# Attention of a hybrid diffusion block: the next unit's scores are written between the second and the third group of turned probabilities

## What is computed

```python
# A, windowed: local keys within +-128 tokens, context keys, a sink
s_loc = einsum('bnqgrd,bnkgd->bngrqk', qb, kb); s_loc = where(mask, s_loc, NEG_INF)
s_ctx = einsum('bnqgrd,bkgd->bngrqk', qb, kc)
p = softmax(concatenate([s_loc, s_ctx, s_sink], -1), -1)
o = p[..., :nk] @ vb + p[..., nk:nk + L] @ vc
# B, neighbourhood: all 512 latent keys with bias and mask, and context keys
s_nb = einsum('brqhd,brwkhd->brhqwk', qg, kg) + bias; s_nb = where(col_ok, s_nb, NEG_INF)
p = softmax(concatenate([s_nb, s_ctx], -1), -1)
# context rows (layer 0 only) attend to the context alone
```

## Time and profile before

| | |
|---|---|
| median of 3 runs | 3837.84 us (3831.02 to 3839.59) |
| profiled execution, time | 3853.39 us |
| profiled execution, span | 3851.7 us |
| TensorE busy | 3421.1 us, 89% of the span |
| VectorE busy | 2324.1 us, 60% |
| ScalarE busy | 1624.9 us, 42% |
| GpSimd busy | 1046.6 us, 27% |
| mean granted TensorE clock | 0.945 |

### The profile page before, as it was taken

How to read it: one execution, slowest core, us unless ns; L and a number is a source line. 1 busy time by engine, 2 the same in 40 slices (tenths; PEclk the granted TensorE clock), 3 DMA queues, 4 the chain that set the end, 5 groups by cost and what they waited for, 6 DMA issues and landing times.

```text
span 3851.7 us, 49012 instructions
## 1 busy us (share of the span) xinstructions
PE 3421.1 (89%) x19072; PEld 2795.1 (73%) x19072; DVE 2324.1 (60%) x3395; ACT 1624.9 (42%) x2095; POOL 1046.6 (27%) x640
## 2 busy tenths in 40 slices
PE   7998898999999869899987299998999959999994
PEld 4997678988887757677766288678766757777773
DVE  2786742511112649999998684833232348998997
ACT  3114743411111246666664322744211126667763
POOL 2001012221211125555553200122222104444442
PEclk8989999999999889999999599998999979999997
DMA  7242133012212439889888122121222219999994
GB/s 242 99 146 80 45 99 121 23 61 88 83 60 83 138 126 308 301 309 311 309 303 291 62 88 77 50 88 44 72 74 90 99 56 314 332 329 341 334 330 177
DMA packets 331926, 633.91 MB, mean 165 GB/s; under 512 B 14526, under 2 KB 104910, under 8 KB 325358
## 3 DMA queue, kind: packets, MB, share of 16 engines
q1 hardware_dynamic: 309056, 557.88, 42.2%
q0 software_dynamic: 22704, 73.73, 5.8%
HBM read 615.05 MB, written 16.50 MB: 164 GB/s over the span
## 4 chain that ended last, share of the span: by engine, by line
PE 64%; DVE 15%; issue 8%; ACT 5%; POOL 3%; DMA 3%; POOLq 1%; DVEq 0%; ACTq 0%; SPq 0%
PE ps L850 41%; PE ps L1256 11%; DVE part L2084 3%; POOL part L796 2%; PE ps L980 2%; PE ps L1012 2%; DVE area L1687 1%; PE ps L998 1%; ACT hx L1527 1%; DVE hx L2084 1%; DMA raw<-in_w_exp_down 1%; ACT area L1379 1%; DVE area L2111 1%; DVE area L2092 1%; PE ps L1000 1%
## 5 line engine op out<-in xcount | busy, mean ns | idle before, releaser
L850 PE MATMUL ps<-hx,part 128*128 128x384 f32 (+2 forms) x4704 | 930.6, 356 | 11.2 <-POOL part L518 5.5
L850 PEld LDWEIGHTS ps<-hx,part 128*128 128x128 f32 x4704 | 831.1, 189 | 99.1 <-issue 23.2
L1256 PE MATMUL ps<-part,hx 128*128 128x512 f32 x3072 | 781.0, 407 | 105.0 <-POOL part L796 72.7
L1256 PEld LDWEIGHTS ps<-part,hx 128*128 128x128 f32 x3072 | 586.4, 195 | 256.5 <-POOL part L796 87.3
L2084 DVE TENSOR_TENSOR part<-raw,part 128x2048 fp32r<-128x2048 f32 (+1 forms) x256 | 587.1, 2296 | 118.1 <-ACT part L1527 115.8
L1527 ACT ACTIVATE part<-raw 128x2048 fp32r<-128x2048 f32 x256 | 490.2, 1916 | 142.7 <-PE ps L1256 119.5
L518 POOL TENSOR_TENSOR part<-raw,part 128x2048 fp32r<-128x2048 f32 x52 | 238.0, 4577 | 821.7 <-ACT part L515 821.6
L1256 PE MATMUL ps<-hx 128*128 128x512 f32 x1536 | 375.0, 393 | 6.6 <-DVE hx L2084 6.4
L1256 PEld LDWEIGHTS ps<-hx 128*128 128x128 f32 x1536 | 289.3, 189 | 75.7 <-DVE hx L2084 8.0
L2084 DVE TENSOR_TENSOR hx<-raw,hx 128x2048 fp32r<-128x2048 f32 (+1 forms) x128 | 308.1, 2407 | 58.9 <-ACT hx L1527 58.3
L850 PE MATMUL ps<-part,hx 128*128 128x256 f32 (+2 forms) x2208 | 317.2, 306 | 18.9 <-DVEq L532 15.5
(11 more groups left out here) (260 smaller groups left out, 3930.2 us busy)
## 6 DMA issues: line engine op xcount, KB each, us to landing
raw<-in_w_exp_gate SPq DMA_DIRECT2D x128, 1024.0 KB, 5.2
raw<-in_w_exp_up SPq DMA_DIRECT2D x128, 1024.0 KB, 5.6
raw<-in_w_exp_down SPq DMA_DIRECT2D x128, 1024.0 KB, 5.2
raw<-in_w_mod SPq DMA_DIRECT2D x48, 1024.0 KB, 6.9
raw<-in_w_in SPq DMA_DIRECT2D x44, 1024.0 KB, 5.4
raw<-in_w_gate SPq DMA_DIRECT2D x32, 1024.0 KB, 8.0
area<-in_bias POOLq DMA_DIRECT2D x32, 512.0 KB, 4.1
raw<-in_w_branch SPq DMA_DIRECT2D x16, 1024.0 KB, 7.3
```

The lines of the kernel that those rows point to most:

```text
L850: last = mm(dst, a, b, start=i == 0, stop=i == len(pairs) - 1)
L1256: last = mm(ps[:, bank, :], x, y, start=kh == 0 and a == 0, stop=kh == 1 and a == len(pairs) - 1)
```

## The change

Only TensorE's program is changed. The bodies of the scores and of one group's transposes become functions, `scores(s)` and `turn_probs(g)`, with the same instructions and waits. The round is written in another order:

```diff
+                for s in range(len(us) + TLAG):
+                    mine = [w for w in range(len(gs)) if gs[w][0] == s - TLAG]
+                    if s >= TLAG:
+                        pe.wait_ge(*S("a_scaled", l).at(s - TLAG + 1))
+                    for g in mine[:2]:
+                        turn_probs(g)
                     if s < len(us):
-                        kind, hh, t = us[s]
-                        (scores of s)
-                    if s >= TLAG:
-                        mine = [w for w in range(len(gs)) if gs[w][0] == s - TLAG]
-                        pe.wait_ge(*S("a_scaled", l).at(s - TLAG + 1))
-                        for g in mine:
-                            (transposes of g)
-                        for g in mine:
-                            values(g)
+                        scores(s)
+                    for g in mine[2:]:
+                        turn_probs(g)
+                    for g in mine:
+                        values(g)
                 st.leave()
```

More of the change, by code:

```diff
@@ L983, in values @@
                     last.then_inc(*S("a_values", l).by(1))
-                for s in range(len(us) + TLAG):
-                    if s < len(us):
-                        kind, hh, t = us[s]
[L988 to L1001, removed]
-                    if s >= TLAG:
-                        mine = [w for w in range(len(gs)) if gs[w][0] == s - TLAG]
-                        pe.wait_ge(*S("a_scaled", l).at(s - TLAG + 1))
-                        for g in mine:
[L1006 to L1014, removed]
-                        for g in mine:
-                            values(g)
@@ new lines, in scores @@
+                def scores(s):
+                    kind, hh, t = us[s]
+                    lo, hi = local_keys(kind, t)
+                    if s >= 1:
+                        pe.wait_ge(*S("a_moved", l).at(s))
+                    qk = []
+                    for h2 in range(2):
+                        hp = slice(h2 * HD, (h2 + 1) * HD)
+                        qk.append((y_v["AB".index(kind)][hp, hh, t * P:(t + 1) * P],
+                                   kA[hp, hh // 2, :] if kind == "A" else kB[hp, hh, :]))
+                    if hi > lo:
+                        for h2, (q, k) in enumerate(qk):
+                            mm(ps[:, h2, 0:hi - lo], q, k[:, lo:hi], start=True, stop=True)
+                    for h2, (q, k) in enumerate(qk):
+                        last = mm(ps[:, 2 + h2, 0:CTX], q, k[:, LAT:TOK], start=True, stop=True)
+                    last.then_inc(*S("a_scores", l).by(1))
@@ new lines, in turn_probs @@
+                def turn_probs(g):
+                    u, b0, nb = gs[g]
+                    if g >= 2:
+                        pe.wait_ge(*S("a_probT", l).at(g - 1))
+                    for b in range(b0, b0 + nb):
+                        for h2 in range(2):
+                            o = (2 * (b - b0) + h2) * P
+                            last = nc.tensor.transpose(ps[:, 4 + g % 2, o:o + P],
+                                                       prob[:, u % NPROB * 2 + h2, b * P:(b + 1) * P], ident)
+                    last.then_inc(*S("a_turned", l).by(1))
```

## The result

The changed kernel takes 3971.42 us (median of 6 runs, 3967.79 to 3983.18) against 3840.92 for the kernel before, timed beside it: ratio 1.0342, 95% interval 1.0325 to 1.0359, so 3.4% or 131 us slower. The profiled execution spans 3967.9 us.

A forecast was written before the change was run, and what follows sets the result against it. TensorE was taken to set the pace before the change, and a ring of scores, VectorE's chain and transposes after it. +101 us for the ring and +30 for the clock on 3837.8 gave about 3968 us, range 3915 to 4015.

The forecast's parts named there:

- The ring: Attention stages: scores, VectorE's chain, wait and transposes form a closed loop one unit long; +101 us at full clock.
- The rounds: Unit times summed from pieces in both layers' branches; a full unit of layer 1's B 6.19 us against 4.88.
- The sum of +101 us: Both attention stages: 21.0 + 27.1 + 33.5 + 24.6 - 5, the added time at TensorE's full clock.
- The clock: TensorE falling to 1.2 GHz after longer idles before transposes, in 27 rounds: +30 us, bounds 0 and 54.
- rival (b): Ring with the clock low in most rounds, B's full units too: 4014 to 4090 us, chance 0.10.
- rival (a): Ring with the clock never falling: 3939 us, chance 0.13.
- The removed wait: Third transposed group's 0.25 us wait for ScalarE's copy, 48 units, 12 us at best; goes and brings nothing.
- Program order: On TensorE matmuls stay in program order, so scores cannot slip past waiting transposes; otherwise the sum would be about zero.
- Sum: Whole kernel: +101 and +30 give +131 us on the median 3837.8, about 3968 us, 3.4% slower.

The follow-up runs named there:

- The extra work on VectorE: One more multiplication by 1.0 on VectorE ahead of the scaling: in the changed kernel 4025.91 us (1.0473), in the kernel before 3858.37 us (1.0047).
- the wait alone: Against the kernel before, only the wait for the scaling moved ahead of the scores, all transposes staying behind them: 3895.54 us, 1.0125.
- the single group: Against the kernel before, the wait and one group of transposes, not two, moved ahead of the scores: 3938.86 us, 1.0252.
- the kernel with six matmuls in the idle: Changed kernel plus six (behind short units) or two matmuls ahead of the scaling wait, only to keep TensorE busy: 3949.10 us, 1.0276.
- the kernel whose round is 4.56 us: Changed kernel with a lag of three units, ScalarE's exponential placed later and the third group's copy between both heads' exponentials: 3818.57 us, 0.9931.

## Why the prediction was right, point by point

**The ring.** The forecast was a wait for scaling of about 1.6 us in full units of B, from a chain of 3.56 us; the trace has 1.57 and 3.56. VectorE's wait for scores, put at 2.3, is 2.49. The extra work on VectorE, the wait alone and the single group show that the ring sets the pace, and that it was the wait's place, with the transposes behind it, that closed it.

**The rounds.** At full clock (the kernel with six matmuls in the idle) they stand against the sums so: full unit of B in layer 1, 6.20 against 6.19; four tiles of layer 1's A, 22.4 (5.43 + 5.30 + 5.78 + 5.90) against 22.34; six of layer 0's A, 29.35 against 29.28; six of its B, 31.4 against 31.31. The sum of +101 us is measured as +105.

**The clock.** Taken as 30 between bounds of 0 and 54, measured as 23 in the total and 24 to 28 in the stages. The direction and the places (tiles 2 and 3 of A, the short units' followers) were right, and the size was a guess between wide bounds that came out well. Of the changed kernel's 27 idles of more than 2.2 us before first transposes, 18 were followed by slow transposes; of the shorter ones none was. Such a fall cost about 1.5 us and not 2.0: in layer 1's A it is 0.88 in the transposes (1.97 for 1.09) and 0.60 up to the end of the scores (1.88 for 1.28), and four tiles take 23.9 us instead of 22.4. In layer 1's full units of B the clock stayed up behind idles of 1.57, as forecast, save in the first two rounds behind A (8.12 and 7.27 us); rival (b) fell there, and rival (a) with the 23 us. The prediction gave the term as 54 by the rule of the Trainium skill ("TensorE: Matmul & The Clock Gate", section "HAM oscillation — how this bites in real kernels"), and that was a misreading. The section ties the fall to waits longer than nearly all idles here, so by it the term would be near nothing. The trace bears out neither: 2.38 us stand before slow transposes and 2.52 before fast ones.

**The removed wait.** The 0.25 before the third group is gone in the trace (0.5 us of waiting for ScalarE left at L1011 in layer 1, 6.0 before) and brought nothing, as said. In the kernel whose round is 4.56 us, with TensorE setting the pace, it is gone as well, and the round is 0.32 under that of before.

**Program order.** That scores do not pass waiting transposes (the Trainium skill, "TensorE: Matmul & The Clock Gate", section "Step-by-step: what each phase is for"): the trace agrees, since the scores at 2610.66 follow the transposes at 2609.63 that had waited 1.57 us.

**Sum.** 3968 forecast, 3971 measured, +131 forecast and +131 measured, where a ring short by 4 us and a clock too dear by about as much cancel. The profiled span grew by 116 only, with the stages at +129: the stages outside the attention took 13 us less in this execution than in that of before, most of it behind the second attention (1289.4 against 1302.2 us). The code of that part is the same in all kernels here, and over the 14 profiled executions it takes between 1289 and 1304 us. The profiled execution of the kernel before, 3853 us, was also slower than any of its six timed runs (3831 to 3843).

## What to carry to other kernels

Before moving a wait on an in-order engine, write down for both engines what stands between the signal and the wait: if the waiting engine's own output feeds the chain that it waits for, the round is as long as the sum of that ring, however idle each engine is. Work that stands between the output and the wait is what hides the chain; an order that takes it away wants one more unit of lag, and each further engine in the round, here ScalarE, has to be put in step as well. Compare the stages' own lengths where the total moves by 10 us for other reasons.

## What the runs showed of the hardware that was not expected

A float32 matmul of 128 columns with weights of 128 by 128 took two instructions and about 0.22 us (a row of 24 instructions took 2.94 us, one of 12, in the kernel with half as many, 1.60), a float32 transpose of the same size one and 0.11; I had put the first at the second's price. With the narrower weights of the values the same two instructions took less: 24 in 1.53 us.

The length of an idle alone did not settle TensorE's clock. In the changed kernel an idle of 2.38 us was followed by 1.2 GHz, and the next one, of 2.52, by full clock:

```profile
2563.89 1.09 PE L1011 MATMUL ps<-consts,area 128*128 128x128 f32 x8 [2.52 <-DVE area L1790]
```

In the kernel with more work on VectorE, idles of 2.16 to 2.17 us in the last 12 full units of B in layer 1 were each followed by eight transposes in 1.09, at full clock:

```profile
2693.86 1.09 PE L1011 MATMUL ps<-consts,area 128*128 128x128 f32 x8 [2.16 <-DVE area L1793]
```

And with the wait alone the clock fell in layer 0's B behind an idle of 1.54 us (and one of 0.69 just before it), no longer than those of 1.57 that left it up in the changed kernel. The context scores behind it took 1.07 us where 0.60 is full clock, and the local scores of the next unit 2.08, not 1.13:

```profile
447.28 1.31 PE L998 MATMUL ps<-area 64*128 64x512 f32 x4 [1.54 <-DVE area L1790]
448.37 1.07 PE L1000 MATMUL ps<-area 64*128 64x256 f32 x4
...
453.05 2.08 PE L998 MATMUL ps<-area 64*128 64x512 f32 x4 [0.76 <-DVE area L1790]
```

What decides between them no run here tells.
